# The second block's modulation sums move from the feed-forward stage into the recurrence's scan

## What is computed

```python
def rwkv7_scan(r, w, k, v, a, b):
    def step(state, inp):                       # for each of 512 tokens, each head
        r_t, w_t, k_t, v_t, a_t, b_t = inp
        sa = jnp.einsum('bhvk,bhk->bhv', state, a_t)
        state = (state * w_t[:, :, None, :] + sa[..., None] * b_t[:, :, None, :]
                 + v_t[..., None] * k_t[:, :, None, :])
        return state, jnp.einsum('bhvk,bhk->bhv', state, r_t)
...
    cond_lat = jax.nn.silu(c)
    cond_ctx = jax.nn.silu(c_ctx)
    for i in range(DEPTH):
        mod = (cond_lat @ ada_w[i] + ada_b[i])[:, None, :]      # ada_w[i]: 1024 x 6144
        modc = (cond_ctx @ ada_w[i] + ada_b[i])[None, None, :]
```

## Time and profile before

| | |
|---|---|
| runs | 4536.22, 4541.85, 4552.05 us |
| profiled execution | span 4542.0 us, 73,530 instructions |
| scan of layer 0 | about 463.8 to 685.5 us |
| scan of layer 1 | about 1825.8 to 2045.6 us |
| feed-forward with the units, layer 0 | 906.3 to 1199.6 us |
| feed-forward with the units, layer 1 | 2264.6 to 2557.9 us |

### The profile page before, as it was taken

The page is one execution under the profiler, slowest core; times in us unless marked ns, Lnnn a source line. Parts: engine busy times, 40 slices in busy tenths (PEclk is TensorE's granted clock), DMA queues, the critical chain, the costliest instruction groups (busy, mean ns, idle before and its releaser), DMA issues.

```text
span 4542.0 us, 73530 instructions
## 1 busy us (share of the span) xinstructions
PE 4202.5 (93%) x32028; PEld 3257.7 (72%) x32028; DVE 1966.0 (43%) x2957; ACT 1514.9 (33%) x2699; POOL 570.2 (13%) x402
## 2 busy tenths in 40 slices
PE   8899779899998999779899998988899999999999
PEld 6676776677776676776677776755688888667877
DVE  4536434455335536434455334357332231443332
ACT  3533233333333533233333333247221121343221
POOL 1215100011002215100011001012000000150000
PEclk9999899899998999999899998999999999999999
DMA  4122002244322132003244321100111111101222
GB/s 159 38 102 70 31 4 93 70 173 172 142 84 104 38 107 70 31 4 107 79 172 167 136 85 41 52 28 1 38 53 64 65 61 61 56 6 61 93 90 92
DMA packets 97681, 351.69 MB, mean 77 GB/s; under 512 B 10064, under 2 KB 13648, under 8 KB 95952
## 3 DMA queue, kind: packets, MB, share of 16 engines
q1 hardware_dynamic: 86480, 313.02, 20.0%
q10 hardware_dynamic: 10880, 33.96, 2.0%
HBM read 332.26 MB, written 14.68 MB: 76 GB/s over the span
## 4 chain that ended last, share of the span: by engine, by line
PE 82%; DVE 7%; ACT 3%; issue 3%; POOL 3%; ACTq 0%; DMA 0%; DVEq 0%; POOLq 0%; SPq 0%
PE ps L350 20%; PE ps L351 19%; PE ps L353 19%; PE ps L1344 7%; PE ps L2370 1%; PE ps L1889 1%; PE ps L391 1%; DVE sml L2445 1%; POOL e L2901 1%; ACT whi L297 1%; PE ps L2814 1%; POOL dd L1194 1%; PE ps L864 1%; POOL ops L1210 1%; POOL ops L1202 1%
## 5 line engine op out<-in xcount | busy, mean ns | idle before, releaser
L307 DVE TENSOR_TENSOR wlo<-ring,whi 128x1024 fp32r<-128x1024 f32 x494 | 623.7, 1263 | 1876.0 <-ACT whi L297 1875.6
L297 ACT CAST whi<-ring 128x1024 fp32r<-128x1024 f32 x494 | 517.4, 1048 | 2139.3 <-PE ps L353 1875.3
L350 PE MATMUL ps<-h_hi,whi 128*128 128x512 f32 x1424 | 597.1, 419 | 16.3 <-DVE h_lo L443 8.9
L351 PE MATMUL ps<-h_lo,whi 128*128 128x512 f32 x1424 | 569.2, 400 | 0.0
L353 PE MATMUL ps<-h_hi,wlo 128*128 128x512 f32 x1424 | 567.9, 399 | 0.0
L350 PE MATMUL ps<-hm_hi,whi 128*128 128x512 f32 (+1 forms) x1408 | 514.4, 365 | 16.5 <-DVE hm_lo L446 15.1
L351 PE MATMUL ps<-hm_lo,whi 128*128 128x512 f32 (+1 forms) x1408 | 480.3, 356 | 0.0
L353 PE MATMUL ps<-hm_hi,wlo 128*128 128x512 f32 (+1 forms) x1408 | 418.5, 355 | 0.0
L350 PEld LDWEIGHTS ps<-h_hi,whi 128*128 128x128 f32 x1424 | 272.9, 192 | 158.7 <-issue 62.4
L350 PE MATMUL ps<-ac_hi,whi 128*128 128x512 f32 x880 | 329.7, 375 | 3.0 <-DVE wlo L307 3.0
L350 PEld LDWEIGHTS ps<-hm_hi,whi 128*128 128x128 f32 x1408 | 267.1, 190 | 86.9 <-DVE hm_lo L446 20.4
(11 more groups left out here) (385 smaller groups left out, 7255.6 us busy)
## 6 DMA issues: line engine op xcount, KB each, us to landing
ring<-in_w SPq DMA_DIRECT2D x590, 512.0 KB, 3.3
h_spill<-h ACTq DMA_DIRECT2D x2, 2048.0 KB, 6.7
x_spill<-x ACTq DMA_DIRECT2D x2, 2048.0 KB, 14.6
m_spill<-m ACTq DMA_DIRECT2D x2, 2048.0 KB, 10.0
h_again<-h_spill ACTq DMA_DIRECT2D x2, 2048.0 KB, 8.9
ma<-m_spill ACTq DMA_DIRECT2D x2, 2048.0 KB, 10.1
x<-x_spill ACTq DMA_DIRECT2D x2, 2048.0 KB, 9.9
x<-in_x SPq DMA_DIRECT2D x4, 512.0 KB, 7.8
```

The lines of the kernel that those rows point to most:

```text
L297: self.A.copy(self.hi[k % 2][:], raw).then_inc(self.s_cut_hi.h, 1)
L307: self.V.tensor_tensor(self.lo[k % 2][:], raw, self.hi[k % 2][:].bitcast(F32), ALU.subtract).then_inc(self.s_cut_lo.h, 1)
L350: T.matmul(ps[:, b, 0:cw], hi, xh(q, c0, cw), start=q == 0, stop=False, skip_group_check=True)
L351: T.matmul(ps[:, b, 0:cw], hi, xl(q, c0, cw), start=False, stop=False, skip_group_check=True)
```

## The change

The units go into the scan. PE issues a unit at the end of places 2 + 23a + (5k)//2, for a = 0, 1, 2 and k = 0 to 7, that is two places in every five. ACT's row copy comes at place 20 + 23a, PE's turning back two places later and DVE's copy one later still. All of them use PSUM bank 6. To have it free, both groups take bank 2 for the products that were in "their" bank 2, in places that don't coincide. Two products move to other banks: the transposed `bar` (now in the group's first bank, from which DVE still reads `bar` and `oe`, so it waits for `oe` and not only for `bar`) and the transposed `v` (now in the second half of the group's second bank, so ACT's copy of the outputs waits for it). The `ada_w` pieces move in the stream, behind the first two pieces of the stage after the scan. These two pieces are cut at place 2 and not 12; the load of `h_again` stays at 12.

```diff
-HYBRID = [(80, "cut"), (16, "cut"), (128, "cut"), (24, "cut"), (192, "cut"), (128, "cut"), (64, "cut"),
-          *[(16, "cut"), (16, "raw")] * FT, *[(24, "cut"), (16, "raw")] * 2, (128, "cut"), (80, "cut")]
+HYBRID = [(80, "cut"), (16, "cut"), (128, "cut"), (24, "cut"), (192, "cut"), (16, "cut"), (384, "raw"), (112, "cut"),
+          (64, "cut"), (16 * FT, "cut"), (8 * FT, "cut"), (80, "cut")]
...
+MOD_FIRST, MOD_SPAN = 2, 23
...
+        mod_pe, mod_act, mod_dve = self.modulation_sums(layer)
+
+        def act_between(i):
+            if i == 2:
+                self.act_cuts(self.held)
+            if i == 12:
+                self.h_again()
+            mod_act(i)
+
+        def dve_between(i):
+            if i == 2:
+                self.dve_cuts(self.held)
+            mod_dve(i)
...
                     for _ in side:
                         more = True
                         break
+            between(k)
...
             if new:
-                dve(c, "my")
-                yield from product("tt", 2, 0, CH, (mat(b, 1), eye), signal=sp)
+                dve(c, "ot")
+                yield from product("tt", 4 * g, 0, CH, (mat(b, 1), eye), signal=sp)
             yield True
             if new:
                 act(c, "tx")
-                dve(c, "ot")
...
             if new:
                 dve(c, "p4")
-                yield from product("dt", 2, 0, CH, (raw(2, c), eye), signal=sx)
+                yield from product("dt", 4 * g + 1, 256, CH, (raw(2, c), eye), begin=not old, signal=sx)
...
             if old:
-                across(c, "yy")
-                A.copy(ops[:, mine, (c - 1) * CH:c * CH], one(1)).then_inc(sa, 1)
+                across(c, "tv" if new else "yy")
+                A.copy(ops[:, mine, (c - 1) * CH:c * CH], one(4 * g + 1)).then_inc(sa, 1)
...
+        unit_at = {MOD_FIRST + MOD_SPAN * a + 5 * k // 2: (a, k) for a in range(3) for k in range(DT)}
+        done_at = {MOD_FIRST + MOD_SPAN * a + 18: a for a in range(3)}
+
+        def unit(a, k):
+            if a == 0 and k == 0:
                 T.wait_ge(self.s_cond.h, 1)
+            if a > 0 and k == 0:
+                T.wait_ge(self.s_mods.h, b_mods + a)
             for g in range(4):
-                T.matmul(ps[32 * g:32 * g + 32, 4 + a % 2, :], self.cond[:, k, :], self.raw_of(steps[4 * i + g]),
+                T.matmul(ps[32 * g:32 * g + 32, 6, :], self.cond[:, k, :], self.raw_of(steps[4 * (DT * a + k) + g]),
                          start=k == 0, stop=k == DT - 1, skip_group_check=True).then_inc(self.s_raw.h, 1)
...
-        def pe_tick(n):
-            if n % 2:
-                mod_pe(n // 2)
-            if n in (18, 34):
-                mod_back(n // 16 - 1)
...
         def down_pe_tick(n):
-            if n < 2:
-                mod_pe(2 * FT // 2 + n)
-            if n == 3:
-                mod_back(2)
...
-        ada = _blocks(f["ada_w_2"][l])
-        for n in range(FT):
-            ws += [up[16 * n:16 * n + 16], ada[16 * n:16 * n + 16]]
-        ws += [down[:24], ada[16 * FT:16 * FT + 16], down[24:48], ada[16 * FT + 16:], down[48:]]
+        gate_b = _tiles(gb)
+        ws += [gate_b[:2 * PIECE], _blocks(f["ada_w_2"][l]), gate_b[2 * PIECE:]]
+        ws += [_tiles(f["w_o_rw"][l]), _tiles(f["w_out"][l])]
+        ws += [_inter(f["w_up"][l][:, :FFN], f["w_up"][l][:, FFN:]), _tiles(f["w_down"][l])]
```

More of the change, by code:

```diff
@@ L1256, in make_spread, with recurrence @@
         return self.s_spr.take(1) + 1
-    def recurrence(self, ready, columns_done):
+    def recurrence(self, layer, ready, columns_done):
         ops = self.view("ops", A1, 5 * DT, S)
@@ L1305, in woven, with scan_pe @@
             yield
-    def scan_pe(self, m, ops, base, ready):
+    def scan_pe(self, m, ops, base, ready, between):
         own = [self.scan_own(g, m, ops, base[g], ready) for g in range(2)]
@@ L1402, in scan_own @@
                 dve(c, "a1")
-                yield from product("tt", 1, 0, CH, (mat("gp", 0), mat("aa")), signal=sp)
+                yield from product("tt", 4 * g + 1, 0, CH, (mat("gp", 0), mat("aa")), signal=sp)
             yield True
@@ L1407, in scan_own @@
                 dve(c, "x4")
-                yield from product("tt", 0, 0, CH, (X, Y), signal=sp)
+                yield from product("tt", 4 * g, 0, CH, (X, Y), signal=sp)
                 dve(c, "p2")
@@ L1420, in scan_own @@
                 dve(c, "a3")
-                yield from product("tt", 1, 0, CH, (mat("gp", 1), mat("aa")), signal=sp)
+                yield from product("tt", 4 * g + 1, 0, CH, (mat("gp", 1), mat("aa")), signal=sp)
             yield True
@@ L1424, in scan_own @@
                 dve(c, "p4")
[L1425 removed]
+                yield from product("tt", 4 * g + 3, 0, 2 * CH, (Pw, mat("oe", slice(0, 2))), signal=sp)
             if old:
                 act(c, "u")
[L1428 removed]
+                yield from product("dd", 4 * g + 1, 0, CH, (mat("st"), raw(0, c - 1)), signal=sp)
             yield True
@@ L1457, in scan_across @@
                     dve(c - 1, "st")
-                yield from product("dt", 0, 0, 2 * CH, (raw(4, c), r_and_a(c)), signal=sx)
+                yield from product("dt", 4 * g, 0, 2 * CH, (raw(4, c), r_and_a(c)), signal=sx)
             yield True
@@ L1480, in scan_across @@
                 own(c, "ya")
-                yield from product("td", 1, 0, CH, (mat("u"), mat(before, 0)), (mat("vt"), mat("kar", 0)), begin=False,
+                yield from product("td", 4 * g + 1, 0, CH, (mat("u"), mat(before, 0)), (mat("vt"), mat("kar", 0)), begin=False,
                                    signal=sx)
@@ L1530, in scan_act @@
                 own(c, "p3")
-                A.copy(m["zz"][:, mine, 2, :], one(0)).then_inc(sa, 1)
+                A.copy(m["zz"][:, mine, 2, :], one(4 * g)).then_inc(sa, 1)
             yield
@@ L1534, in scan_act @@
                 own(c, "u")
-                A.copy(m["u"][:, mine, :], one(1)).then_inc(sa, 1)
+                A.copy(m["u"][:, mine, :], one(4 * g + 1)).then_inc(sa, 1)
             yield
@@ L1575, in with_rr @@
             own(c, name)
-            V.tensor_tensor(m["aa"][:, mine, :], one(1), m["rr"][:, mine, :], ALU.add).then_inc(sv, 1)
+            V.tensor_tensor(m["aa"][:, mine, :], one(4 * g + 1), m["rr"][:, mine, :], ALU.add).then_inc(sv, 1)
         for c in range(NCH + 1):
@@ L1899, in pe_back, with pe, act, dve @@
             m.then_inc(self.s_mback.h, 1)
-        def act(a):
-            A.wait_ge(self.s_raw.h, steps[4 * (DT * a + DT - 1) + 3].value)
-            if a == 2:
-                A.wait_ge(self.s_mback.h, b_back + 1)
-            A.copy(row[a % 2][:], ps[:, 4 + a % 2, :]).then_inc(self.s_mrow.h, 1)
-        def dve(a):
-            V.wait_ge(self.s_mback.h, b_back + a + 1)
-            out = self.mod_sums[:, layer, 16 * a:16 * a + 16, :].rearrange("p (g q) c -> p q g c", q=4)
-            V.tensor_copy(out, ps[:, 6, 0:32].rearrange("p (q g c) -> p q g c", q=4, g=4)).then_inc(self.s_mods.h, 1)
-        return pe, pe_back, act, dve
+        def pe(i):
+            if i in unit_at:
+                unit(*unit_at[i])
+            if i - 2 in done_at:
+                back(done_at[i - 2])
+        def act(i):
+            if i in done_at:
+                a = done_at[i]
+                A.wait_ge(self.s_raw.h, steps[4 * (DT * a + DT - 1) + 3].value)
+                if a == 2:
+                    A.wait_ge(self.s_mback.h, b_back + 1)
+                A.copy(row[a % 2][:], ps[:, 6, :]).then_inc(self.s_mrow.h, 1)
+        def dve(i):
+            if i - 3 in done_at:
+                a = done_at[i - 3]
+                V.wait_ge(self.s_mback.h, b_back + a + 1)
+                out = self.mod_sums[:, layer, 16 * a:16 * a + 16, :].rearrange("p (g q) c -> p q g c", q=4)
+                V.tensor_copy(out, ps[:, 6, 0:32].rearrange("p (q g c) -> p q g c", q=4, g=4)).then_inc(self.s_mods.h, 1)
+        return pe, act, dve
     def conv_ffn(self, layer, b_lo):
```

86 lines of the change are left out of this document (31 added, 55 removed).

## The result

| | before | changed |
|---|---|---|
| median of the runs | 4540.11 us | 4552.69 us |
| lowest to highest | 4532.14 to 4552.05 | 4547.35 to 4561.89 |
| profiled execution, span | 4542.0 us | 4547.7 us |

The ratio is 1.0030, with an interval of 1.0021 to 1.0038. The kernel is slower by 13.6 us (10 to 17), where 4522 us and a gain were forecast. The profiled executions differ by only 5.7 us, so stages are compared by them, and whole kernels by the ratios.

The account below looks back on a forecast made before the run. PE, busy for 93% of the span, was taken as the bound. Feed-forward -52 - 5, scan +52 + 4 + 2.5 + 1, taken up -30, `oe` +4, cuts -3, instructions +6 gave -20.5 us: 4522 us, range 4499 to 4550.

Parts of the forecast that it names:

- Feed-forward, -57 us: Feed-forward: 48 units of 1.09 us (52 us) and six turnings back (5 us) leave PE, all gained.
- Rival (d): Feed-forward: the cuts become its bound and a fifth of 57 us is lost, 4533 us; chance 0.09.
- The units and what the idle time takes up, +59.5 - 30 = +29.5 us: Scan: units +52, slow start +4, turnings back +2.5, copies +1; PE's idle time takes up 15 us in a layer.
- The doubled cost in the slow start: Scan's first 25 us, clock 0.59: the first two units each cost up to 1.09 us more, +4 us (0 to 4).
- rival (a): Scan: it swallows nearly everything, 46 of 52 us, 4506 us, or 4500 with no late instructions; chance 0.15.
- `oe` and the cuts at place 2, +4 - 3 = +1 us: Scan: transposed `bar` waits for `oe`, +4 us; cuts moved from place 12 no longer hold PE up, -3 us.
- Instructions, +6 us (0 to 40): Scans: about 100 instruction transfers, some later beside the raw pieces, each costing 0 to 1.06 us if meeting a weight transfer.
- Rival (c): Scan: instructions late beside weights, 0.6 us per transfer, +60 us, 4576 us; issue waits over 40 us a scan; chance 0.10.
- A wait of PE for a piece of the ring: Scan: priced at nothing; its appearance would show the forecast wrong altogether.
- the scans grew by 29 and 22 us and not by 18: Sign for the scan: it grows from 222 and 220 us by some 18 us in each layer.
- the idle time did not fall to 33 us: Sign for the scan: PE's idle time falls from 47 us to some 33 us.

Follow-up runs that it names:

- e3_resident: The changed kernel with the units' matmuls reading constants in SBUF and no raw pieces streamed: 4498.57 us, ratio 0.9908 to before.
- e2_no_sums: The changed kernel with its banks and cuts, but no units and no raw pieces: 4493.89 us, ratio 0.9891 to before.
- e10: As e9, with every gated load held 128 instructions longer: 4541.64 us, ratio 1.0003 to before.
- e9: As e5_places, PE's program unchanged, loads of raw pieces 5 to 48 of each scan held until 20 of 256 instructions past a block's edge: 4510.23 us, ratio 0.9943.
- e5_places: The changed kernel without the bound on the cuts' look-ahead, units at places 1, 3 and 5 of each eight: 4543.55 us, ratio 1.0009 to before.
- e12_first_free: As e9, but the gates on loads begin with piece 13 of each scan: 4505.17 us, ratio 0.9928 to before.

## Why the prediction was wrong

The ladder by the ratios, each step times 4540 us: no sums in the feed-forward, the new banks and cuts -49.5; the units +7.7; their stream +43.1; the late cut +12.3; sum +13.6. Each kernel's ratio is known to 4 to 6 us, so the small steps are rough. Of the stream's step 38 us lie in the two scans: 28 us more idle time, and 10 us more busy time, at granted clocks of 0.94 and 0.96 where e3_resident has 0.97 and 0.97.

**Feed-forward, -57 us.** Right: -27.9 us in each layer, -55.8 us, with PE busy for all but 1.2 of 264 us, and the cuts did not become its bound. Rival (d) is out.

**The units and what the idle time takes up, +59.5 - 30 = +29.5 us.** Mis-sized to the safe side. Units, turnings back, copies and the slow start cost 8 us together (e2_no_sums to e3_resident). PE's idle time gave 16 us per scan, where 15 was forecast. The rest is the clock. PE's busy time grew by 22 us in layer 0 (173.1 to 194.7) and 19 us in layer 1 (176.0 to 195.0), against the 26 that I had carried over from the feed-forward's columns and the turnings back and the slow start on top. But the granted clock of the scans rose with it, from 0.94 and 0.93 to 0.97. Busy time times clock, an estimate of the work at the full clock, grew by 26.5 and 25.3 us: the units cost what was forecast, and the fuller scan ran faster, which no term of mine had. The doubled cost in the slow start didn't come either; the clock in it is 0.59 without units and 0.80 with them in e3_resident, 0.73 in the changed kernel. For the sum, rival (a) had this right, but in part by luck: it had all of it from idle time.

**`oe` and the cuts at place 2, +4 - 3 = +1 us.** Right: 2 us in the scans, within the noise. (The ladder's first step is 6 us short of the feed-forward's 55.8; the rest lies in steps of 1 to 4 us in stages that the change doesn't touch.)

**Instructions, +6 us (0 to 40).** This is the step that failed. It named the right resource and had the price at the wrong end. I argued that a transfer can lose at most its own length, 1.06 us, and only with a chance of 0.38, the DMA share. Both are wrong. The transfer isn't stretched by one packet. Mostly it stands behind the burst that was issued before it, which lasts 2.1 us for one piece and 3.1 to 5.3 for two. And the chance isn't the share of time: with bursts in the same share of it, twice as many transfers meet one in e10 as in e9. By the estimate above PE has some 0.2 us to spare before it stops at record 193, so nearly all of a delay counts. The runs show 43 us for the stream (46 with e5_places' units, of which 37 go when only the moments of the loads change, e5_places to e12_first_free). Rival (c) had the mechanism and a threshold of 0.4 us per transfer; 43 us over 104 transfers are 0.41 us. It had a chance of 0.10. Its waits by issue, over 40 us in a scan, did not come: they stood at 27 and 23.

The prediction weighed the Trainium skill's DMA: Bandwidth & Descriptors (section on queues, rings and completion order), by which an engine takes its queues in turn, packet by packet. If that packet were one of the profile's, 4 KB and 0.16 us in the median, a transfer would not be 1 to 1.5 us late. But the page gives its packet 9 to 17 descriptors, and a piece is 128 packets of 4 KB in the profile, 8 for each of 16 DMA engines, so one packet of the page may be a whole piece's share, which takes 2.1 us. Read so, e10's bursts of one piece agree with it, and so do the 8 of 42 in the changed kernel. It does not fit where PE had stopped at record 193 before the transfer started: at 606.49 that is 0.6 us behind the stop and, from record 28 on, some 3.2 us late by the estimate above, longer than one piece takes. The rule of Runtime: NRT & Kernel Launch (section on instruction fetch mechanics), which has a block's crossing mostly hidden, holds neither before (16.9 us) nor after (26.9 us).

**What was missing.** The late cut, +12 us. I priced the cuts' move from place 12 to 2 and asked whether the ring keeps up in the scan, but not what the place of 48 pieces in the stream does to the planner's look-ahead, which counts in pieces of the stream. The order of ACT's program shows it before any run: three cuts in a row where there was one behind each column. "A wait of PE for a piece of the ring" was named as what would make the forecast wrong; the wait came, for the cut of a piece and not in the scan but behind it.

The sum was 34 us off: 37 us of it are the stream and 12 us the late cut, and the other terms, 15 us better than forecast, hid a part of that.

Of what was to show the steps: the feed-forward shrank as said; the scans grew by 29 and 22 us and not by 18; the idle time did not fall to 33 us, but to that very level (31.3) without the stream; the issue waits stood at 27 us in layer 0, between the 17 of before and (c)'s 40.

## What to carry to other kernels

- Work moved from a dense stage into one that runs short on instructions brings its data with it. Ask what else uses the DMA engines there, above all the engine's own instructions, and price a late transfer with the burst that stands before it, not with a packet. If it can't be avoided, gate the loads: one small load in each block of 256 instructions, timed to run behind the transfer, gave 37 us here without touching PE's program.
- Idle time that looks like waits for other engines can be filled well: 24 units of 1.09 us each made a scan of 220 us 4 us longer on average, 16 us of them lying in idle time and 5 to 6 us given back by a higher granted clock.
- Where one table orders a stream, read every place that measures a distance in it, and look at the other engines' order behind the moved work, not only at the engine that it was moved on.

## What the runs showed of the hardware

- A transfer of 16 KB of PE's instructions that falls due in a burst of weights mostly starts near the burst's end or just behind it (38 of 50 in its last 0.5 us or behind in e10, 32 of 42 behind 1.75 or more of two pieces in the changed kernel); PE goes on 1.2 to 1.7 us after the transfer's end.
- PE ran out of instructions at one point of every block: all 418 stops of over 0.5 us that end by issue, in the scans of 14 kernels, begin 193 records past a multiple of 256.
- Four matmuls with 32 columns of weights each, to four groups of 32 partitions, take 1.06 us; two of them take 1.05 us.
- The granted clock in the scan's first 25 us was 0.59 without units and 0.73 with the first three of them in it. Over a whole scan it was 0.93 to 0.95 without units, 0.97 with units of 512 columns and no stream, and with the stream 0.86 and 0.92 with units of 32 columns against 0.95 and 0.96 with units of 512.
